# MLP up projection of two transformer blocks with weight blocks stationary and both parts of the tokens in one moving run

## What is computed

```python
# block 1; block 2 is the same with norm2_g, w_mlp_in, w_mlp_out
h = rms_norm(x, norm_mlp_g) @ w_mlp_up          # 256 x 2048 @ 2048 x 8192
x = x + jnp.square(jax.nn.relu(h)) @ w_mlp_down # 256 x 8192 @ 8192 x 2048
```

## Time and profile before

| | us |
|---|---|
| three runs, median (lowest to highest) | 3125.66 (3124.02 to 3125.87) |
| the profiled execution, its own time | 3126.18 |
| its span in the trace | 3124.5 |
| TensorE busy, matmuls | 3086.4 (99%) |
| VectorE busy | 1939.6 (62%) |
| ScalarE busy | 1407.0 (45%) |
| GpSimd busy | 471.3 (15%) |

### The profile page before, as it was taken

The page is one execution under the profiler, slowest core; times in us unless marked ns, Lnnn a source line. Parts: engine busy times, 40 slices in busy tenths (PEclk is TensorE's granted clock), DMA queues, the critical chain, the costliest instruction groups (busy, mean ns, idle before and its releaser), DMA issues.

```text
span 3124.5 us, 37766 instructions
## 1 busy us (share of the span) xinstructions
PE 3086.4 (99%) x13866; PEld 2505.3 (80%) x13866; DVE 1939.6 (62%) x2100; ACT 1407.0 (45%) x1649; POOL 471.3 (15%) x430
## 2 busy tenths in 40 slices
PE   8999999999999999999999999999999999999998
PEld 6777888888888888888876668888888888888887
DVE  5566654556776665566677775655555556655666
ACT  5445544445444444444533446444444444444443
POOL 2000100117880000000046550100000000000000
PEclk9999999999999999999999999999999999999999
DMA  6544666656666666666754445666656666666664
GB/s 198 155 142 145 217 191 202 201 177 219 213 206 220 187 190 188 188 189 191 228 165 152 145 135 174 208 211 205 210 191 188 189 188 191 187 189 189 190 188 148
DMA packets 297646, 585.34 MB, mean 187 GB/s; under 512 B 18520, under 2 KB 18688, under 8 KB 297152
## 3 DMA queue, kind: packets, MB, share of 16 engines
q1 hardware_dynamic: 291328, 562.11, 58.4%
q0 software_dynamic: 6080, 21.70, 2.3%
q10 hardware_dynamic: 128, 0.03, 0.0%
HBM read 571.19 MB, written 12.58 MB: 187 GB/s over the span
## 4 chain that ended last, share of the span: by engine, by line
PE 93%; DVE 3%; issue 2%; ACT 1%; DMA 0%; DVEq 0%; SPq 0%; ACTq 0%
PE banks L1488 91%; PE banks L1491 2%; DVE wlo L939 1%; ACT whi L552 0%; ACT W L552 0%; DVE W L1309 0%; DVE W L1314 0%; DMA raw<-in_w_in 0%; ACT XH L552 0%; DVE W L1306 0%; DVE W L1305 0%; ACT G L552 0%; DVE W L1381 0%; DVE W L1388 0%; DVE W L1112 0%
## 5 line engine op out<-in xcount | busy, mean ns | idle before, releaser
L939 DVE TENSOR_TENSOR wlo<-raw,whi 128x1024 fp32r<-128x1024 f32 x1048 | 1363.3, 1307 | 973.9 <-ACT whi L552 967.2
L552 ACT ACTIVATE whi<-raw 128x1024 fp32r<-128x1024 f32 x1048 | 1101.4, 1059 | 1199.6 <-PE banks L1488 1136.3
L1488 PE MATMUL banks<-whi,Y 128*128 128x512 f32 x4800 | 1497.0, 391 | 1.8 <-DVE W L1388 1.7
L1488 PEld LDWEIGHTS banks<-whi,Y 128*128 128x128 f32 x4800 | 901.1, 188 | 189.8 <-issue 2.9
L1488 PE MATMUL banks<-wlo,Y 128*128 128x512 f32 x2400 | 934.0, 389 | 0.0
L1488 PE MATMUL banks<-whi,XH 128*128 128x512 f32 x1792 | 717.6, 400 | 15.5 <-DVE wlo L939 12.9
L1488 PE MATMUL banks<-whi,XL 128*128 128x512 f32 x1792 | 700.7, 391 | 0.0
L1488 PE MATMUL banks<-wlo,XH 128*128 128x512 f32 x1792 | 700.4, 391 | 0.0
L1488 PEld LDWEIGHTS banks<-wlo,Y 128*128 128x128 f32 x2400 | 450.8, 188 | 91.8
L1488 PEld LDWEIGHTS banks<-whi,XH 128*128 128x128 f32 x1792 | 337.6, 188 | 111.3 <-issue 26.0
L1488 PEld LDWEIGHTS banks<-whi,XL 128*128 128x128 f32 x1792 | 337.3, 188 | 73.2
(11 more groups left out here) (250 smaller groups left out, 1246.7 us busy)
## 6 DMA issues: line engine op xcount, KB each, us to landing
raw<-in_w_in SPq DMA_DIRECT2D x384, 512.0 KB, 3.9
raw<-in_w_mlp_up SPq DMA_DIRECT2D x128, 512.0 KB, 3.8
raw<-in_w_mlp_down SPq DMA_DIRECT2D x128, 512.0 KB, 3.7
raw<-in_w_mlp_in SPq DMA_DIRECT2D x128, 512.0 KB, 3.8
raw<-in_w_mlp_out SPq DMA_DIRECT2D x128, 512.0 KB, 3.7
raw<-in_w_branch SPq DMA_DIRECT2D x80, 512.0 KB, 4.2
raw<-in_w_out SPq DMA_DIRECT2D x64, 512.0 KB, 4.5
tables<-G POOLq DMA_DIRECT2D x8, 1024.0 KB, 8.3
```

The source lines that it names most:

```text
L552: return nc.scalar.activation(out_, in_, f, **kw)
L939: tt(wlo[:, i % RING, :], raw[:, i % RING, :], whi[:, i % RING, :].bitcast(F32), ALU.subtract)\
L1488: return nc.tensor.matmul(out_, l, r, start=start, stop=stop, **kw)
```

## The change

- **Up projection** (`up_unit`): the weights are stationary and the tokens move. A unit goes through the four blocks f of 128 hidden channels and the two k-tiles. `whi`'s block is loaded and multiplied with 512 columns, high and low part of all 256 tokens side by side (MX); then `wlo`'s block with the 256 columns of the high part. That is 8 matmuls of 512 columns and 8 of 256, each with its own weight load. The result has hidden channels on partitions, in four banks: columns 0 to 255 and 256 to 511 of a bank have yet to be added.
- **Hidden layer**: ScalarE copies the right halves of the four banks to HSUM (`low_half`); VectorE adds the left halves (`summed`) and then writes HSQ = max(HSUM, 0) * HSUM; ScalarE rounds it to the high part (`hidden_hi`), VectorE writes the low part (`hidden_lo`). No transposes.
- **Norm**: the inverse root is no longer applied in relu. Its square, r2, is applied to the down projection's result, in the addition to x (`down_add`).
- **Banks**: the up chunks use PU and PT, four banks; the first one uses both pairs of PA, and waits in the middle of its first unit (`half`) until `out` 3 has been added to x.
- The wait for the tables is gone, and the loop of TensorE takes in the chunk that was written out behind it.

The diff, cut:

```diff
-        HB = [tok(slot(W, 4 + i)) for i in range(2)]
+        HSUM, HSQ = ft(slot(W, 4)), ft(slot(W, 5))
+        MX = Y[:, 0:2 * KD * T].rearrange("p (k n) -> p k n", n=2 * T)
+        HID = [[Y[:, SL * (i + h):SL * (i + h + 1)].rearrange("p (k t) -> p k t", t=T) for h in range(2)] for i in (8, 0)]
...
-                hi_, m = (XH if ph == "a" else YH), norms[b, ph]
+                hi_, m = (XH if ph == "a" else MX[:, :, 0:T]), norms[b, ph]
...
+                def hidden_hi(j, to=0):
+                    act.wait_ge(S(f"square{b}_ready"), j + 1)
+                    if not to:
+                        act.wait_ge(used, mlp_base(b, j))
+                    a(HID[to][0], HSQ).then_inc(S(f"hidden{b}_hi"), 1)
+
+                def low_half(base, s, d, n):
 
                     act.wait_ge(used, base + 8)
-                    for t in range(NT):
-                        ins = a(HB[0][:, t, :], acc[t], ACT.Relu, scale=rs[:, t:t + 1])
-                    ins.then_inc(S(f"relu{b}_ready"), 1)
+                    a(HSUM[:, d:d + n, :], banks[:, s:s + n, T:2 * T]).then_inc(S(f"low_half{b}"), n // 2)
...
-                    for i in range(7):
+                    for i in range(6):
                         hi(base, i)
-                    split_pair(j, 0)
-                    split_pair(j, 1)
-                    for i in range(7, 12):
+                    hidden_hi(j)
+                    for i in range(6, 12):
                         hi(base, i)
-                    relu(base, j + 1)
+                    low_half(base, 4, 0, 4)
...
+                low_half(u0[b, "m"], 2 * first_up(b), 0, 2)
+                low_half(u0[b, "m"], 2 - 2 * first_up(b), 2, 2)
...
-                def square(n):
-                    dve.wait_ge(S(f"relu{b}_ready"), n + 1)
-                    tt(HB[1], HB[0], HB[0], ALU.mult).then_inc(S(f"hidden{b}_ready"), 1)
+                rs = RS[norms[b, "m"]]
+
+                def summed(j):
+
+                    n = 0 if isinstance(j, int) and j == -1 else j + 1
+                    if isinstance(j, int) and j == -1:
+                        for i, s in enumerate((2 * first_up(b), 2 - 2 * first_up(b))):
+                            dve.wait_ge(S(f"low_half{b}"), i + 1)
+                            h = HSUM[:, 2 * i:2 * i + 2, :]
+                            tt(h, banks[:, s:s + 2, 0:T], h, ALU.add).then_inc(S(f"up{b}_read"), 1)
+                    else:
+                        dve.wait_ge(S(f"low_half{b}"), n * 2 + 2)
+                        tt(HSUM, banks[:, 4:8, 0:T], HSUM, ALU.add).then_inc(S(f"up{b}_read"), 2)
+                    dve.wait_ge(S(f"up{b}_read"), n * 2 + 2)
+                    stt(HSQ, HSUM, 0.0, HSUM, ALU.max, ALU.mult).then_inc(S(f"square{b}_ready"), 1)
+
+                def hidden_lo(j, to=0):
+                    dve.wait_ge(S(f"hidden{b}_hi"), j + 1)
+                    tt(HID[to][1], HSQ, HID[to][0].bitcast(F32), ALU.subtract).then_inc(S(f"hidden{b}_split"), 1)
...
-                    for t in range(NT):
-                        x = X[:, t, CH * n:CH * n + CH]
-                        ins = tt(x, PA[n % 2][t], x, ALU.add)
-                    ins.then_inc(evict["dve"], 1)
-
-                def split_pair(j, r, to=0):
-                    kt = KD + 4 * to + UK * r
-                    split_lo(j * 2 + (H0 + r), r, YH[:, kt:kt + UK, :], YL[:, kt:kt + UK, :])
+                    down_add(n)
...
                     lo(base, 2)
+                    if first:
+                        summed(-1)
...
-                    if first:
-                        square(0)
-                    else:
+                    if not first:
                         add(last, 3)
                     for i in range(4, 7):
                         lo(base, i)
-                    split_pair(j, 0)
-                    split_pair(j, 1)
+                    hidden_lo(j)
                     for i in range(7, 12):
                         lo(base, i)
-                    square(j + 1)
+                    summed(j)
...
+                dve.wait_ge(S("rs_ready"), norms[b, "m"] + 1)
+                chain(tt(r2, rs, rs, ALU.mult))
...
-                if b != blocks[-1]:
-                    dve.wait_ge(S("tables_saved"), 32 * S5_TILES // TG)
-                split_pair(NF - 1, 0, 1)
-                split_pair(NF - 1, 1, 1)
+                hidden_lo(NF - 1, 1)
...
+            def down_add(n):
+                for t in range(NT):
+                    x = X[:, t, CH * n:CH * n + CH]
+                    ins = stt(x, PA[n % 2][t], r2[:, t:t + 1], x, ALU.mult, ALU.add)
+                ins.then_inc(evict["dve"], 1)
...
+            def up_unit(base, i, k0, acc, first, last, half=None):
+
+                pe.wait_ge(lo_done, base + (i + 1))
+                for f in range(4):
+                    if f == 2 and half is not None:
+                        pe.wait_ge(*half)
+                    for k in range(UK):
+                        c = slice(CH * k + P * f, CH * k + P * f + P)
+                        mm(acc[f], whi[:, i % RING, c], MX[:, k0 + k, :], start=first and k == 0,
+                           stop=last and k == UK - 1, skip_group_check=True)
+                        ins = mm(acc[f][:, 0:T], wlo[:, i % RING, c], MX[:, k0 + k, 0:T], start=False,
+                                 stop=last and k == UK - 1, skip_group_check=True)
+                ins.then_inc(used, 1)
...
-                def split(j, r):
-                    pe.wait_ge(ts_split, j * 2 + (H0 + r - 1))
-                    pair(None, r, HB[1], 2 * P * r)
...
-                    pe.wait_ge(ts_split, j * 2 + (H0 + 2))
+                    pe.wait_ge(S(f"hidden{b}_split"), j + 1)
                     for i in range(8):
                         n = i // 2
                         if i % 2 == 0:
                             pe.wait_ge(evict["dve"], j * 4 + (e0 + n - 1))
-                        unit(base, i0 + i, YH, YL, KD + 4 * at + UK * (i % 2), PA[n % 2], i % 2 == 0, i % 2 == 1)
+                        unit(base, i0 + i, HID[at][0], HID[at][1], UK * (i % 2), PA[n % 2], i % 2 == 0, i % 2 == 1)
...
-                def body(j, more=()):
+                def body(j):
                     base = mlp_base(b, j)
                     if not (isinstance(j, int) and j == 0):
-                        pe.wait_ge(S(f"relu{b}_ready"), j + 1)
-                    for i in range(4):
-                        unit(base, i, YH, YL, UK * i, PU, i == 0, False)
-                    pe.wait_ge(S(f"hidden{b}_ready"), j + 1)
-                    split(j, 0)
-                    split(j, 1)
-                    for i in range(4, 8):
-                        unit(base, i, YH, YL, UK * i, PU, False, i == 7)
-                    down(j, base, 8, 0, more)
+                        pe.wait_ge(S(f"up{b}_read"), j * 2 + 2)
+                    for i in range(8):
+                        up_unit(base, i, UK * i, PU + PT, i == 0, i == 7)
+                    down(j, base, 8)
 
                 body(0)
-                with pe.Fori(1, NF - 2) as j:
+                with pe.Fori(1, NF - 1) as j:
                     body(j)
-                body(NF - 2, [Steps(last_pairs())])
+                pe.wait_ge(S(f"up{b}_read"), 2 * NF)
...
-                    unit(0, u0[b, "m"] + i, YH, YL, UK * i, PA[first_up(b)], i == 0, i == 7)
+                    half = (evict["dve"], find[(b, "out", 3)].evicted) if i == 0 else None
+                    up_unit(0, u0[b, "m"] + i, UK * i, PA[first_up(b)] + PA[1 - first_up(b)], i == 0, i == 7, half)
```

More of the change, by code:

```diff
@@ L117, in build @@
         D_KR, D_KI = vec(32), vec(32)
+        r2 = vec(2)
         def slot(t, i, n=1):
@@ L198, in build @@
             ts0[b] = ts
-            ts += 24 + 2 * NF
+            ts += 24
         evict = {"act": S("acc_read_by_act"), "dve": S("acc_read_by_dve")}
@@ L858, in body @@
                         hi(base, i)
-                    split_pair(j, 0)
-                    split_pair(j, 1)
-                    for i in range(7, 12):
+                    hidden_hi(j)
+                    for i in range(6, 12):
                         hi(base, i)
-                    relu(base, j + 1)
+                    low_half(base, 4, 0, 4)
                     for i in range(12, 16):
                         hi(base, i)
-                for i in range(4):
+                for i in range(3):
@@ L879, in mlp @@
+                low_half(u0[b, "m"], 2 - 2 * first_up(b), 2, 2)
+                for i in range(3, 6):
+                    hi(mlp_base(b, 0), i)
+                hidden_hi(0)
+                for i in range(6, 12):
+                    hi(mlp_base(b, 0), i)
+                low_half(mlp_base(b, 0), 4, 0, 4)
                 for i in range(12, 16):
-                    hi(base, i)
+                    hi(mlp_base(b, 0), i)
                 with act.Fori(1, NF - 1) as j:
                     body(j)
-                split_pair(NF - 1, 0, 1)
@@ L884, in mlp @@
-                split_pair(NF - 1, 1, 1)
```

(30 more changed lines are left out.)

12 lines of the change are left out of this document (1 added, 11 removed).

## The result

The changed kernel takes 3133.84 us (median of 10 runs, 3131.95 to 3136.51) where the kernel before takes 3125.72 (10 runs, 3123.54 to 3126.89): the ratio is 1.0028, with an interval of 1.0019 to 1.0036. It is slower by 8 us where 18 us of gain were forecast. The profiled execution took 3136.51 us (span 3134.8; before 3126.18 and 3124.5). What follows explains the 10.3 us between the two spans and, more than that, the 28 us between sum and span.

What follows compares the result with a forecast made beforehand. TensorE, 99% busy, was taken as the bound. Terms of -28.2 + 1.0 + 5.5 + 3.9 = -17.8 us took 3126.2 to 3108 us, with a range of 3098 to 3121.

Steps and rivals of the forecast that it cites:

- 2: Up units recast with half their matmuls at 256 columns: 2048 of these at 0.1139 us each, 1.0 us more.
- first rival: Up units: a 256-column matmul doesn't hide the load behind it; fully 3261 us, mostly 3110 to 3150; chance 0.08.
- Step 1: MLP chunks of both blocks: removing 256 transposes shortens TensorE's chain by 0.88 us per chunk, 28.2 us less.
- last rival: Transposes in the MLP cost less than their length because TensorE would wait otherwise, so the 28 us don't come; chance 0.02.
- second rival: Up units: every weight load is exposed, 116 us more than the forecast, 3224 us; chance 0.01.
- Step 3: First up chunk of each block: TensorE waits for `out` 3 to be added to x, 5.5 us more.
- Step 4: Hidden layer: VectorE gets more work per chunk, 29.4 of 43.5 us, but nothing on the path in the steady state.
- Step 5: Block 1's first three chunks, beside GpSimd: VectorE's sum delays the adds that TensorE waits for, 3.9 us more.
- Step 6: Costed at nothing: the wait for the tables, r2, the loop's extra chunk, DMAs and the tail after the last chunk.

Runs made afterwards that it cites:

- e5: The changed kernel with the weight loads that run under the short matmuls in up cut from 128 to 64 columns; 3114.07 us.
- e8: The kernel before with two transposes per chunk instead of eight; 3105.56 us beside 3125.95 us.
- e4: The changed kernel with the addition of `out` 3 to x behind one low part instead of three; 3132.08 us.
- e1: Runs of eight: the changed kernel with each up unit's eight 512-column matmuls first, then its eight of 256, instead of alternating; 3127.27 us.

## Why the prediction was wrong

The step that failed is **2, "I take 0.1139: 2048 x 0.0005 = 1.0 us more"**. It measured 2048 x 13 ns = 27 us: short matmuls in turn with long ones, under full loads, are not as quick as their columns. The mechanism was named, as the first rival, with the point at 8.7 ns from which it decides and "10 to 30 ns, so 3110 to 3150" as its likely size; the value was 13 and the time 3134. It had a chance of 0.08. The readings that this rested on were each of another thing. The earlier trace rows have loads of 8 columns, and the load is half of the cause: with 64 columns under the short matmul there is no excess (e5), with 96 there is. The earlier trace rows have full loads under short passes, but four equal ones in a row; and runs of eight show that equal neighbours cost 120 ns and not 113, while unequal neighbours cost the long ones as well. Neither row had long and short in turn with full loads, which is the one pattern that the change makes, 2048 times. The lower end of the term, 7 us of gain, rested on one rounded reading of 0.11. The upper end allowed 3.6 us, as if the cost could only come at the starts of units.

The trace of before also held a sign. Each time that TensorE's even pace of 227 ns is broken in the MLP, by transposes or a wait, the next distances are uneven. Behind the transposes of a steady chunk they are so for two matmuls and for nine by turns, 10 and 41 ns in all beyond the pace; the longer series is 229, 233, 236, 224, 231, 236, 228, 233, 231 and then 227. The 233, 236, 228, 232, 231 behind a change of length in runs of eight is much alike. A stream that needs several matmuls to settle may never settle where each differs from the last; that this is the cause of the 13 ns is not shown.

**Step 1** was right: the removal of three quarters of the transposes alone brought 20.4 of the 21 us expected (e8), and the last rival falls. **The second rival** (every load exposed) falls too: it asked for 116 us more, and the chunk grew by 0.85 us beyond its columns, which is 27 us in all.

**Step 3**: 4.5 us idle instead of 5.5, in the place given. What was missing is the clock: block 2 pays some 2 us more behind the stall (e4). No term of the prediction charged the clock. In block 1 the early add brought nothing, since the time was then waited for elsewhere.

**Step 4** was right. The add on PSUM takes 743 ns, the three new instructions 1217 to 1225, and no wait ends with them in the steady state. VectorE's groups from 970 to 1360 us, beside the earlier trace rows:

```profile
L1433 DVE SCALAR_TENSOR_TENSOR W<-banks,small,W 128x512 f32<-128x512 f32 x72 | 50.5, 743 | 0.0
L1386 DVE SCALAR_TENSOR_TENSOR W<-W 128x1024 f32<-128x1024 f32 x9 | 11.0, 1225 | 0.3
L1384 DVE TENSOR_TENSOR W<-banks,W 128x1024 f32<-128x1024 f32 x9 | 11.0, 1217 | 0.0
L1390 DVE TENSOR_TENSOR Y<-W,Y 128x1024 fp32r<-128x1024 f32 x8 | 9.7, 1218 | 0.0
```

**Step 5**: 3.9 us forecast; the waits for the add grew from 1.7 to 5.0, 3.3 more. The chain at the second of them shows the low parts in GpSimd's stretch, 2.70 and 2.07 us for what takes 1.23 elsewhere, ahead of the adds:

```profile
931.34 2.70 DVE wlo L934
...
934.68 2.07 DVE wlo L934
...
937.52 1.41 DVE W L1433 x2
```

And the 3.5 us wait that ends at 939.05 was followed by the lower clock, 2.4 us more. By the Trainium skill ("SBUF — State Buffer", "SBUF: two separate sides") a VectorE instruction with two SBUF inputs and a GpSimd instruction that reads SBUF can't hold the port pair that they share at the same time, and one waits for the whole of the other. The 2.70 us are consistent with that; no run here takes GpSimd away, so it is not shown. **Step 6**: nothing came of it.

So the sum by the prediction's terms as measured is -28.2 + 27 + 4.5 + 3.3 = +6.6. The clock adds 2 in block 2 and 2.4 in block 1 and takes off the 1.5 between the MLPs, and 1.2 were there before the MLP began: +10.7, against 10.3 between the spans.

**What stays open** is the mechanism inside TensorE. The runs show its conditions and not its cause: it needs full loads and unequal lengths; shortening either of the two loads to 64 columns halves it or more, though this also narrows what is written; it isn't monotonic in the short one's length (8.9 ns at 288, 11.4 at 320); at the lower clock it isn't seen in the five pairs that ran there (427 and 213 ns).

## What to carry to other kernels

Before a stream of equal matmuls is broken into long and short ones, find the exact alternation with full loads in a trace, or measure it: the same number of columns is not the same time, and 13 ns for each of 2048 pairs ate a saving of 28 us. If short ones are needed, put equal ones side by side (13 to 8 ns here). A change that puts a short stall into TensorE's stream should be charged with the clock behind the stall as well as the stall: here 2 us behind 2.3 and 2.4 behind 3.5, in some executions and not in others.

## What was not expected of the hardware

- Unequal neighbours: 236 + 117 ns for 512 + 256 columns with loads of 128 x 128, 227 + 113 with loads of 64 columns ahead of the long one, 427 + 213 at 1.2 GHz.
- An even stream of 256-column matmuls with full loads runs at 119 to 120 ns, not 113 (e1).
- The same stall of 2.3 us was followed by the lower clock in block 2 (0.79 over 8 us) and not in block 1; in four other runs with that stall it was in block 1 too (0.50 from 788.5 to 791 us).
- By the Trainium skill ("TensorE: Matmul & The Clock Gate", Part 3, "What overlaps and what doesn't") a weight load overlaps a running matmul only when the row group differs. The run with all matmuls of 512 columns does not agree: every load there uses all rows, and the matmuls are 227 ns apart with a full load for each.
